# Block sums of a modulation vector: one wide VectorE operation per load, gathered in 2 KB pieces

## What is computed

```python
def ada_modulation(cond, w, b):
    m = jax.nn.silu(cond) @ w + b          # w: (2048, 6 * 2048), N_MOD = 6
    return jnp.split(m[..., None, :], N_MOD, axis=-1)

# first block: proj = rms_norm(x) @ w_in; 8 heads of attention; a gated short convolution; x += y @ w_out
# second block, for x:
sh_a, sc_a, g_a, sh_m, sc_m, g_m = ada_modulation(c, w_ada[layer], b_ada[layer])
h = modulate(rms_norm_2(x, norm_attn_w[layer]), sh_a, sc_a)      # h * (1 + sc_a) + sh_a
x = x + g_a * (concatenate([attn, pool]) @ w_out[layer])
hm = modulate(rms_norm_2(x, norm_mlp_w[layer]), sh_m, sc_m)
x = x + g_m * squared_relu_mlp(hm, w_mlp_up[layer], w_mlp_down[layer])
```

## Time and profile before

| | |
|---|---|
| time, median of 3 runs | 1686.93 us (1685.69 to 1689.96) |
| the profiled execution | 1685.83 us |
| its span in the trace | 1683.8 us |
| mean granted TensorE clock | 0.986 of full speed |
| busy: PE, DVE, ACT | 1602.2, 1197.8, 765.7 us |
| heads, convolution bodies, output projection | about 25 to 265, 265 to 483, 483 to 585 us |
| DMA moved | 374.74 MB, mean 223 GB/s |

### The profile page before, as it was taken

One profiled execution on the slowest core, in us unless ns is written; L12 is line 12 of the kernel. 1 busy time (PEld: TensorE's weight loads), 2 busy tenths in 40 slices (PEclk: granted clock), 3 DMA queues, 4 the chain that ended last, 5 costly groups with the idle time before them and its releaser, 6 DMA issues.

```text
span 1683.8 us, 33301 instructions
## 1 busy us (share of the span) xinstructions
PE 1602.2 (95%) x12150; PEld 1489.6 (88%) x12150; DVE 1197.8 (71%) x1791; ACT 765.7 (45%) x1055; POOL 33.9 (2%) x50
## 2 busy tenths in 40 slices
PE   3999999999999989988899999999999999999996
PEld 2999998899989978887799998899988998899985
DVE  5777777788888775676766666776678666556675
ACT  4545444344444543443455454345533554345441
POOL 0000000000000000000000100000000000000000
PEclk9999999999999999999999999999999999999998
DMA  7878887788966667533165457885698556655552
GB/s 308 308 271 295 285 285 270 288 312 326 338 245 204 226 234 290 210 101 101 63 189 185 153 183 234 268 262 184 186 285 265 187 178 189 191 162 180 186 187 87
DMA packets 94264, 374.74 MB, mean 223 GB/s; under 512 B 9984, under 2 KB 10512, under 8 KB 83424
## 3 DMA queue, kind: packets, MB, share of 16 engines
q1 hardware_dynamic: 88368, 335.97, 60.0%
q10 hardware_dynamic: 4608, 33.56, 5.6%
q0 software_dynamic: 1200, 4.02, 0.7%
HBM read 371.40 MB, written 2.10 MB: 222 GB/s over the span
## 4 chain that ended last, share of the span: by engine, by line
issue 73%; PE 19%; DVE 7%; ACT 1%; POOL 0%; POOLq 0%; DVEq 0%; ACTq 0%
PE G L425 5%; PE G L427 5%; PE G L426 5%; DVE lo L1172 1%; DVE blk L1172 1%; PE M L704 1%; PE ADA L467 1%; DVE sm L1511 1%; DVE blk L1524 1%; PE S L678 1%; PE ADA L718 1%; ACT hi L834 1%; DVE t L1221 0%; DVE resid L1704 0%; PE S L691 0%
## 5 line engine op out<-in xcount | busy, mean ns | idle before, releaser
L1172 DVE TENSOR_TENSOR lo<-raw,hi 128x1024 fp32r<-128x1024 f32 x496 | 607.6, 1225 | 222.8 <-ACT hi L834 213.0
L834 ACT ACTIVATE hi<-raw 128x1024 fp32r<-128x1024 f32 x496 | 526.1, 1061 | 504.1 <-PE G L427 270.9
L425 PE MATMUL G<-actA,hi 128*128 128x256 f32 (+1 forms) x2368 | 683.0, 288 | 16.5 <-DVE actA L1172 16.5
L426 PE MATMUL G<-actA,lo 128*128 128x256 f32 (+1 forms) x2368 | 670.6, 283 | 0.0
L427 PE MATMUL G<-actA,hi 128*128 128x256 f32 x2368 | 670.3, 283 | 0.0
L425 PEld LDWEIGHTS G<-actA,hi 128*128 128x128 f32 x2368 | 450.5, 190 | 49.8 <-issue 31.9
L426 PEld LDWEIGHTS G<-actA,lo 128*128 128x128 f32 x2368 | 450.7, 190 | 0.3
L427 PEld LDWEIGHTS G<-actA,hi 128*128 128x128 f32 x2368 | 450.1, 190 | 0.0
L451 PE MATMUL G<-actB,hi 128*128 128x512 f32 x1024 | 356.8, 392 | 2.8 <-DVE lo L1172 2.8
L452 PE MATMUL G<-actB,lo 128*128 128x256 f32 x1024 | 287.5, 281 | 0.0
L451 PEld LDWEIGHTS G<-actB,hi 128*128 128x128 f32 x1024 | 192.3, 188 | 45.2 <-issue 3.1
(11 more groups left out here) (200 smaller groups left out, 1167.8 us busy)
## 6 DMA issues: line engine op xcount, KB each, us to landing
raw<-stream_dram SPq DMA_DIRECT2D x496, 512.0 KB, 4.3
ada_raw<-w_ada_dram SPq DMA_DIRECT2D x64, 1024.0 KB, 7.7
ada_raw<-w_ada_dram ACTq DMA_DIRECT2D x32, 1024.0 KB, 5.9
x_tok<-x_tok_dram SPq DMA_DIRECT2D x1, 2048.0 KB, 8.3
resid<-xT_dram SPq DMA_DIRECT2D x1, 2048.0 KB, 11.7
ctx_tok<-ctx_tok_dram SPq DMA_DIRECT2D x1, 2048.0 KB, 18.5
W<-ctxT_dram POOLq DMA_DIRECT2D x16, 128.0 KB, 3.4
out_dram<-resid SPq DMA_DIRECT2D x4, 512.0 KB, 2.7
```

The source lines that it names most:

```text
L425: pe.matmul(wide, hi[:, slot, cols], x[:, k, 0:T + extra], start=(k == 0), stop=False, skip_group_check=True)
L426: pe.matmul(wide, lo[:, slot, cols], x[:, k, 0:T + extra], start=False, stop=False, skip_group_check=True)
L834: return act.activation(dst, src, ACT.Copy)
L1172: return dve.tensor_tensor(dst, a, b, op)
```

## The change

The block sums take a load per *contraction tile* in place of one per 512 columns. Load n of a block holds contraction tile n for all 2048 columns, so DVE needs one operation of 2048 columns with one scalar per partition, and `part` is 2048 wide. In memory these are four pieces of 2 KB per partition, taken from four rows of `w_ada` that lie 4 MB apart (the same expression as in `gate_load`). The partitions are added once per block of 16 takes, with 16 products: in body 8 and behind unit 3 of the output projection. Take 31 moves from lap step 3 to step 1 of the first `out_lap`, and the last `part_add` from behind all four laps to behind the first. `part` moves into the room of `y_conv`, since `y_attn` and `y_conv` shrink to one tile each. Number, size (1 MB) and place of the loads stay.

```diff
-        part = sb("part", [P, 512])
-        y_attn, z_attn, y_conv, z_conv = (mix1[:, i] for i in range(4))
+        z_attn, z_conv = mix1[:, 1], mix1[:, 3]
+        y_attn, y_conv = mix1[:, 0, 0:1], mix1[:, 0, 1:2]
+        part = mix1[:, 2].rearrange("p k t -> p (k t)")
-        PART = S[0][:, 3 * P:3 * P + 4]
+        PART = S[0][:, 3 * P:3 * P + KT]
...
             def part_sums(n):
-                pe.wait_ge(ada_taken, 4 * (n + 1))
+                pe.wait_ge(ada_taken, KT * (n + 1))
                 if n:
                     pe.wait_ge(part_added, n)
-                for m in range(4):
-                    x = pe.matmul(PART[:, m:m + 1], part[:, m * P:(m + 1) * P], ones[:, 0:1], start=(m == 0), stop=(m == 3),
+                for m in range(KT):
+                    x = pe.matmul(PART[:, m:m + 1], part[:, m * P:(m + 1) * P], ones[:, 0:1], start=(m == 0), stop=(m == KT - 1),
                                   skip_group_check=True)
...
# PE, head_body
-                if prev and h % 2 == 0:
-                    part_sums(h // 2 - 1)
# PE, conv_body
-                if h % 2 == 0:
-                    part_sums(h // 2 - 1)
+                if tail:
+                    part_sums(0)
# PE, output projection
-                if n == 5:
-                    part_sums(7)
+                if n == 3:
+                    part_sums(1)
...
-            def part_load(n, row):
-                act.wait_ge(ada_taken, n)
-                src = t_in["w_ada"][row] if isinstance(row, int) else t_in["w_ada"][bass.ds(row, 1)].rearrange("a p n -> (a p) n")
-                act.dma_start(ada_raw[:, 1].rearrange("p k n -> p (k n)"), src).then_inc(ada_full[1], 16)
+            def part_load(n):
+                if n:
+                    act.wait_ge(ada_taken, n)
+                block, m, g = 2 + n // KT, n % KT // 4, n % 4
+                src = t_in["w_ada"][block * KT:(block + 1) * KT].rearrange("(n m) p (g c) -> m g p n c", m=4, g=4)[m, g]
+                act.dma_start(ada_raw[:, 1], src).then_inc(ada_full[1], 16)
...
             def part_take(n):
-                if n % 4 == 0 and n:
-                    dve.wait_ge(part_summed, n // 4)
+                if n == KT:
+                    dve.wait_ge(part_summed, 1)
                 dve.wait_ge(ada_full[1], 16 * (n + 1))
-                k = n % 4 * 4
-                for m in range(4):
-                    w, c = ada_raw[:, 1, m, :], cpad[:, k + m, 6:7]
-                    if k + m == 0:
-                        seq(dve.tensor_scalar(part[:], w, c, None, ALU.mult))
-                    elif m < 3:
-                        seq(dve.scalar_tensor_tensor(part[:], w, c, part[:], ALU.mult, ALU.add))
-                    else:
-                        dve.scalar_tensor_tensor(part[:], w, c, part[:], ALU.mult, ALU.add).then_inc(ada_taken, 1)
-                        own(ada_taken)
+                w, c = ada_raw[:, 1].rearrange("p k n -> p (k n)"), cpad[:, n % KT, 6:7]
+                if n % KT == 0:
+                    dve.tensor_scalar(part, w, c, None, ALU.mult).then_inc(ada_taken, 1)
+                else:
+                    dve.scalar_tensor_tensor(part, w, c, part, ALU.mult, ALU.add).then_inc(ada_taken, 1)
+                own(ada_taken)
...
# DVE: part_add(n) now adds KT columns; it stands in conv_body 8 and behind the first out_lap
-                if prev and n % 2 == 0:
-                    part_add(n // 2 - 1)
-                if n % 2 == 0:
-                    part_add(n // 2 - 1)
+                if tail:
+                    part_add(0)
-                    if j == 3 and first:
+                    if j == 1 and first:
                         part_take(2 * KT - 1)
             out_lap(At(U_OUT1), 0, True)
+            part_add(1)
             with turn.lap(dve, 3, "dve w_out") as i:
                 out_lap(At(U_OUT1 + 4, 4, i), i + 1)
-            part_add(7)
```

More of the change, by code:

```diff
@@ L904, in head_body @@
                 if n:
-                    part_load(2 * n, 2 * KT + 2 * n)
+                    part_load(2 * n)
                 if prev is not None:
@@ L927, in head_body @@
                 split(at, 3, 0)
-                part_load(2 * n + 1, 2 * KT + 2 * n + 1)
+                part_load(2 * n + 1)
                 if prev is not None:
@@ L937, in conv_body @@
                 at = At(4 * n)
-                y = y_conv[:, 0:1] if tail else y_conv[:, i:i + 1]
+                y = y_conv
                 if block is not None:
@@ L960, in conv_body @@
                 if tail:
-                    head_out(y_attn[:, HEADS - 1:HEADS])
+                    head_out(y_attn)
                 act.wait_ge(x_new, turn.next("x_new"))
@@ L1004, in _ @@
                 act.wait_ge(act_seq, turn.next("seq"))
-            act.dma_start(ada_raw[:, 1].rearrange("p k n -> p (k n)"), t_in["w_ada"][2 * KT]).then_inc(ada_full[1], 16)
+            part_load(0)
             head_body(0, None)
             for n in range(1, HEADS):
-                head_body(n, y_attn[:, n - 1:n])
+                head_body(n, y_attn)
             conv_body(8, True, None, 0)
@@ L1255, in part_take @@
             def part_take(n):
[L1257 to L1258 removed]
+                if n == KT:
+                    dve.wait_ge(part_summed, 1)
                 dve.wait_ge(ada_full[1], 16 * (n + 1))
[L1260 to L1269 removed]
+                w, c = ada_raw[:, 1].rearrange("p k n -> p (k n)"), cpad[:, n % KT, 6:7]
[4 more added lines that the diff above has]
+                own(ada_taken)
             def part_add(n):
                 dve.wait_ge(part_summed, n + 1)
[L1274 to L1275 removed]
+                at = (2 + n) * KT
+                tt(adav[:, 0, at:at + KT], PART, col("b_ada", at, KT), ALU.add).then_inc(part_added, 1)
                 own(part_added)
```

10 lines of the change are left out of this document (4 added, 6 removed).

## The result

| | before | after |
|---|---|---|
| median | 1687.41 us | 1730.51 us |
| profiled execution | 1685.83 us | 1732.77 us |
| its span | 1683.8 us | 1730.7 us |
| busy PE, DVE | 1602.2, 1197.8 us | 1622.5, 1175.3 us |
| mean granted TensorE clock | 0.986 | 0.976 |

The change makes the kernel 2.55% slower (ratio 1.0255, 95% interval 1.0238 to 1.0271), 43 us by the medians. I had forecast 1700.8 us, with 1712 at the head of the range: the direction was right, the size was not.

What follows compares the result with a forecast made beforehand. PE was taken to bound the convolution stretch, with a low-slack load loop behind it. Loop +12.3, sums on PE +2.2 and waits -0.6 gave +13.9 us on 1686.9: 1700.8 us, range 1683.7 to 1712 (forecast's own 1690 to 1712).

Steps and rivals of the forecast that it cites:

- The loop: Convolution stretch, loads 17 to 30: issue, landing and DVE take through one buffer would bind, 177.0 to 189.3 us, +12.3 us.
- L: Time from a block-sum load's issue to DVE's take, taken as 9.1 us, with bounds 6.1 and 9.9.
- Heads: Head bodies: later loads and shorter takes stay hidden behind DVE's 1.46 us idle after an even take; 0 us.
- What bounds the kernel: From 300 to 400 us PE bounds, busy 98.41 of 100 us; a DVE gain is nearly all off the path.
- break-even: In the convolution stretch, L = 8.2 us makes the loop equal the present 177.0 us; below it PE bounds again.
- Narrow to wide: DVE takes: one 2048-column operation of 2352 ns for a 3.11 us chain, 0.75 us less each, off the path except in the loop.
- Sums on PE: Partition sums in heads, body 8 and output projection: 2 x 16 matmul pairs for 8 x 4, together +2.2 us.
- Rival A: Block-sum loads with L under 8.2 us: pieces hidden, PE still bounds, -3.2 us, 1683.7 us; chance 0.30.
- Rival B: Convolution stretch: DMA engines full, at most 292 GB/s, +17 us, 1705.5 us; chance 0.10, together with L over 10.5.
- The rule that speaks against this: Block-sum loads: skill asks only 512 B for line rate, so pieces free; its 4 MiB pitch estimate, 10 us, agreed only in direction.

Runs made afterwards that it cites:

- contiguous variant: Changed kernel with each block-sum load laid out as one run of 8 KB per partition, all else of the change kept: 1688.22 us, ratio 1.0015.
- the split: Changed kernel with contiguous loads and each group of 16 partition sums split in two groups of 8: 1684.04 us, ratio 0.999 against the kernel before.
- two-buffer variant: Changed kernel, gather kept, with a second buffer for even loads, each load waiting only for the take before last: 1697.11 us, ratio 1.0063.

## Why the prediction was wrong, point by point

Of the 46.9 us, 13.9 were forecast. The mechanism of the loop was right and its load latency L too small (13.1 us), the heads were put at nothing (about 16), and what waits cost PE in clock was in no term.

- **What bounds the kernel:** right. PE at clock 1.00 and idle for only 1.6 of 100 us, one loop of waits with very little slack.
- **The loop:** mechanism right, size off. The mis-sized term is L: 9.1 taken, 9.8 to 10.0 measured, and with it the +12.3 us, for which 25.4 were measured. The formula 14 L + 61.9 stands: 200.5 for L = 9.9 beside 202.4 measured. I had moved away from the median of the gate loads because ACT's queue seemed worth 1.7 us. The rows had said no such thing for gathered loads, and SP's 8 KB loads beside them are later too. With the median of the nearest row (9.9) the term would have been 23.5. The break-even at L = 8.2 agrees with the variants, though none lies near it: in the table all with a landing of 6.5 to 7.3 us lie at 1687.6 to 1693.4 us, those with 9.8 at 1730.
- **Heads: 0.** This step failed. It measured about +15 us (+14.7 with the gather in the heads alone; +16.7 up to the issue of load 17, where -0.8 stood). "After an even take DVE idles 1.46 us" was true, but it was the cover of the wrong take: the odd take stands ahead of the softmax scale, for which PE waited 0.60 us already. A wait that is in the list of before has no slack at all; that row was on my page and I used it as a gain. It weighs more than the 13.1 us by which the loop was too small.
- **Narrow to wide:** right, 2352 ns. With the rest of the change around it, it is worth 15 us with slow loads and nothing with quick ones. The first of a block (multiplication alone), which I had priced the same, takes 1286 ns.
- **Sums on PE: +2.2.** Too small, as price per product: 16 took 298.59 - 293.11 = 5.48 us in body 8 of after and 3.5 in the contiguous variant, 3.2 forecast. In body 8 of after they began 1.5 us after a wait of 0.98 us had ended, and the steps behind them are 0.21 us, the lower clock:

```profile
293.11 5.62 PE L486 MATMUL S<-ones,mix 128*128 128x1 f32 x32
298.59 0.56 PE L426 MATMUL G<-actA,hi 128*128 128x256 f32 x1
```

  And bunched, they themselves cost clock afterwards, some 3.4 us that no term held. That is also why rival A's 1683.7 did not come with quick loads but only with the split (1684.0). That the two agree to 0.3 us is partly luck: of the 3.2 us of rival A, the wait of 1.4 us for `ss` did not go away in either variant.
- **Waits for nothing new (clock):** no step of mine said what an idle PE costs beyond its idle time. 27.0 us of new waits came with an estimated 18 us of lower clock.
- **Rival A** (pieces hidden): its condition, L under 8.2, was a matter of the address pattern, which I had held for fixed by "2 KB". **Rival B** (DMA engines full): its sign is there, with 8 to 9 us of the 43 by the two-buffer variant, though not as an alternative but on top. I had made the two exclude each other, and so the range ended at 1712.
- **The rule that speaks against this:** I had set the rule on 4 MiB pitches of the Trainium skill, "DMA: Bandwidth & Descriptors", aside since its estimate didn't fit the gate rows. As a cause it was the right one: padding by 4 KB took most of the loss away. The 9.9 us of the gate loads fit this pattern's own time, and on ACT's queue it was 9.8.

What is not settled: why exactly 4 or 8 MB, an 8 KB step and a quarter read must come together. The runs show the combination and not its cause. With a quarter read, 1, 2, 4 and 8 MB were tried; other distances, and other steps than 2 and 8 KB, were not. And the two 4 KB variants differ from the changed kernel by half of each 8 KB read in place of a quarter, but also by two pieces per partition in place of four; which of the two made them quick isn't separated, so "a quarter read" stands for both.

## What to carry to other kernels

Before a load is gathered, look at the addresses and not only at the piece size: if the pieces stand an exact large power of two apart (here 4 or 8 MB) and only a small part of each step is read (here a quarter in four pieces; half in two pieces was quick), pad the rows by a few KB (here 43 us became 7). A transfer on a one-buffer loop is paid in full on every pass above its break-even, so price it by the median of the nearest row, and look for slack behind *every* place at which the loop touches an engine's order, beginning with the waits that the list shows already. When many tiny matmuls are to run in a row, spread them between large ones; it cost nothing here and mostly paid.

## What the runs showed of the hardware

- Loads of 1 MB in 2 KB pieces exactly 4 or 8 MB apart, with 8 KB from partition to partition: 9.8 us to landing; exactly 1 or 2 MB, or 4 MB + 4 KB: 7.2, 7.2 and 7.1. The same 16,896 packets fill the engines for 9.9% of the span in after and 6.2% with 4 MB + 4 KB. With 4 KB pieces 4 or 8 MB apart: 7.3 and 7.1 us.
- Slow loads on one queue delay the others: SP's 8 KB loads took 10.4 us for 7.9, the stream's halves 8.9 for 5.9 (300 to 500 us).
- The granted clock of TensorE falls to its lower level behind waits (3.31 us idle: steps of 0.21 for 0.12 us right behind it), and in most traces also behind 3.5 us of one-column products in which PE isn't listed as idle (0.96 and 0.91 over the stretches around them, but 1.00 in one trace). Split in groups of 1.7 us with no wait before them, these left it at 1.00 (contiguous and padded). The Trainium skill, "TensorE: Matmul & The Clock Gate", section "What's actually happening", has the clock follow how busy the array is; the fall behind the wait agrees, the one behind one-column products, for which PE is listed as busy all the time, is not to be read from it.
